# One core, two transformer blocks: the transposed copies of the second direction's inverse are taken by VectorE, and the attention's parts are dealt out in twos and ones

## The chip, the core and the metric

The kernel runs on one core of a Trainium2 chip. A core has five engines that run side by side and meet only in semaphores: TensorE (PE, matmuls, with PEld for its weight loads), VectorE (DVE), ScalarE (ACT), GpSimd (POOL) and SyncE (SP, which here only issues DMAs). Matmuls write PSUM (eight banks of 128 partitions by 512 float32), VectorE and ScalarE carry results from there to SBUF. The metric is device time in microseconds, lower is better: the median of the runs. Before the change three runs gave 1783.94 us (1781.68 to 1788.37).

## The reference

Two blocks follow each other. The first is a two-layer token mixer with pooling, dilated attention and a convolutional feed-forward net, over 256 tokens of width 1024. The second takes its output together with 256 context tokens and computes

```
h   = rms_norm(x) * (1 + scale) + shift;      p = h @ w_in            # for latents and context
a   = hgrn2_mixer(...)                        # gated linear attention, 4 heads, both directions
b   = rwkv7_mixer(...)                        # delta rule, 4 heads of 64, both directions
c   = neighbourhood_attention(...)            # 8 heads of 64, window and context keys, softmax
x   = x + g1 * (concat(a, b, c) @ w_out)
x   = x + g2 * hierarchical_moe(rms_norm(x))  # 32 experts, weights of some 200 MB
```

The delta rule is a recurrence over 512 tokens in each direction (context first, then latents):

```
sa = s @ kk_t
s  = s * w_t - sa * ak_t + v_t * k_t
y  = s @ r_t
```

The change touches b for the second direction (backwards over the tokens) and the order in which b and c are interleaved. Nothing of what is computed changes.

## The kernel before

**The tiles.** The delta rule is computed in chunks of 64 tokens, eight to a direction. Four groups g = 2*dr + pr hold the two directions dr and the two pairs of heads pr. For each chunk and head the kernel needs the inverse X of a unit triangular 64x64 matrix (made of LT) and its transpose XT. It is built up in levels: blocks of 2, 4, ... 64 rows. A level n has two stages of the list GROUP_STAGES (line 242 on):

- `MXn`: TensorE computes T1 = LT times X (`to_heads`, its records stand at L1649) and turns X with four transposes (`turned`, L1639; the job is named XV). T1 and XV are carried from PSUM to SBUF: w.T1 and w.XT, each 128x512 float32, by ScalarE (`take`, L2371).
- `XMXn`: TensorE waits for both copies and computes the update XU (`to_parity`, L1622; in the last level XTU by `heads64`, L1612), and VectorE merges it into X or XT under a mask (`copy_predicated`, L3069 and L3071).

Before the levels stands `products` (L1632, L1622, L1612), behind them `G`, `H` and `Psi`, whose products are taken by ScalarE too; in H, TensorE waits for G's take before it multiplies PH. The last result is GT of group 3, which the state recurrence behind the mixer (L1938) and the weight stream wait for.

**The attention.** "near" is the neighbourhood attention: eight pairs p of two heads, six parts each, 50 steps in all (`NA_STEPS`), done one part at a time:

- part 0: TensorE computes the logits ns of both heads (L1758), VectorE scales the first head's, adds the bias, finds the maximum and negates it (L2968, L2970, L2972, L2973). It waits until the previous pair has left the buffer nL, that is for the transposes nt.
- part 1: VectorE does the second head's logits; ScalarE takes the exponential of the first (L2410); TensorE computes the previous pair's output no (L1766), which VectorE copies (L2982).
- part 2: ScalarE, exponential of the second head. Part 3: VectorE, the reciprocal of the sums (L2986). Part 4: ScalarE scales both heads (L2416). Part 5: TensorE transposes the probabilities, nt (L1774), and ScalarE takes them (L2371).

**The order.** Every engine runs its instructions in the order of its program. `mixer_steps()` writes one list, MIXER_STEPS, which all the engines walk: the 56 steps of `GROUP_STEPS` (for each direction, for each stage, pair of heads 0, then 1), and behind step n so many attention parts as `NEAR_AT[n]` says. Steps 0 to 27 are the first direction, steps 28 to 55 the second. `group_jobs()` lists the PSUM results of a stage with the engine that empties each; from it `taken_order()` counts the semaphore values and `second_banks()` deals the PSUM banks (a job takes the bank whose last user is emptied first in the list). TensorE's `fill` waits for the earlier users of the bank.

**Behind the mixer** SyncE waits until GT of group 3 is in PSUM and then loads w_out (L1284), and after it the experts' weights in blocks of 2 MB (L1312), each as soon as the place it goes to is free; some of the places are held by the rest of the mixer, up to L3221, L3238, L3250 and L3263. The mixture of experts works through eight turns of four experts with these blocks.

Of the kernel before, what the change touches and what calls it, by code (L numbers as in the profile page):

```python
# [187 lines left out]
NCH = T2 // CH  # L188
# [54 lines left out]
GROUP_STEPS = [(stage, 2 * dr + pr) for dr in range(2) for stage in GROUP_STAGES for pr in range(2)]  # L243
# [7 lines left out]
def mixer_steps():  # L251
# [27 lines left out]
    for n, group_step in enumerate(GROUP_STEPS):  # L279
# [5 lines left out]
        if group_step == ("MX2", 1):  # L285
            steps.append(("vtok", 0))
        for _ in range(NEAR_AT[n]):
            steps.append(("near", i))
# [5 lines left out]
NA_PAIRS, NA_PARTS = 8, 6  # L294
NA_STEPS = NA_PAIRS * NA_PARTS + 2
ROPES_AT = {2: 0, 4: 1, 6: 2, 8: 3}
NEAR_AT = [int(n > 8 and n % 2 == 1) if n < 28 else 1 + int(n % 5 in (0, 3)) for n in range(len(GROUP_STEPS))]
MIXER_STEPS = mixer_steps()


def group_jobs(stage, g):

    if stage == "gates":
        return [("wz", g, "act"), ("az", g, "act")]
    if stage == "products":
        return [("LT", g, "act"), ("L1", g, "act"), ("ta", g, "act"), ("M2T", g, "dve"), ("tk", g, "act"), ("tkk", g, "act"),
                ("NN", g, "dve")]
    if stage == "G":
        return [("W2", g, "act")]
    if stage == "H":  # L310
        return [("G", g, "act"), ("H", g, "act"), ("HN", g, "act"), ("PH", g, "dve")]
    if stage == "Psi":
        return [("PS", g, "act"), ("GT", g, "act")]
    n = int(stage[-1])
    if stage[0] == "M":
        return [("T1", 8 * g + n, "act"), ("XV", 8 * g + n, "act")]
    return [("XU", 8 * g + n, "dve")] if n < 5 else [("XTU", 8 * g + n, "dve")]


# [193 lines left out]
def build(nc, d, out):  # L513

    ctx = ExitStack()
    with ctx:
# [3 lines left out]
        def sem(name):  # L520
            return ctx.enter_context(nc.semaphore(name))
# [76 lines left out]
        act = R[:, mark:mark + FT * S].rearrange("p (f s) -> p f s", s=S)  # L598
# [310 lines left out]
        w = ahead[0]  # L909
# [3 lines left out]
        w = ahead[1]  # L913
# [8 lines left out]
        def inputs_of(g):  # L922

            return (work if g < 2 else ahead)[g % 2]
# [55 lines left out]
        dve_emptied2 = sem("dve_emptied2")  # L980
# [29 lines left out]
        def wait_full2(eng, job):  # L1010

            eng.wait_ge(full2, JOB2[job] + 1)

        def wait_emptied2(eng, job):

            who, n = EMPTIED2[job]
            eng.wait_ge(act_emptied2 if who == "act" else dve_emptied2, n)
# [1118 lines left out]
        def _(act_eng):  # L2136
# [41 lines left out]
            for l in range(DEPTH):  # L2178
# [30 lines left out]
                else:  # L2209
                    for j in range(4):  # L2210
                        t, half = j // 2, j % 2
# [28 lines left out]
                for g in range(4):  # L2240
                    b = bank[JOB[("pool", g)] % 4]
# [35 lines left out]
                for j in range(11):  # L2277
                    wait_full(a, l, ("up", j))
                    high(l, SPLIT[("up", j)] + 2)
                    b = bank[JOB[("up", j)] % 4]  # L2280
# [41 lines left out]
            for j in range(4):  # L2322
                t, c = j // 2, slice((j % 2) * 512, (j % 2 + 1) * 512)
# [8 lines left out]
            def full_bank(job):  # L2332
                wait_full2(a, job)
                if job[0] in PLACE:
                    return place2(*job)
                return pair2(*job) if job[0] in QUADS else bank2(*job)
# [19 lines left out]
            def take(job, dst, func=ACT.Copy, scale=1.0, n=512, split=None):  # L2356
                b = full_bank(job)
                if job[0] in PLACE:
                    dst = dst.rearrange("p (n b) t -> p b n t", b=2)
                elif job[0] == "L1":  # L2360
                    dst, b = dst.rearrange("p (n b) t -> p b n t", b=2), b.rearrange("p b (n t) -> p b n t", t=64)
                elif job[0] in QUADS:
                    dst = dst.rearrange("p (b n) t -> p b (n t)", b=2)
                elif job[0] == "XV":
                    dst = dst.rearrange("p (b n) t -> p n b t", b=2)
                    b = b.rearrange("p (n b t) -> p n b t", n=NCH // 2, b=2)
                else:
                    b = b[:, 0:n]
                    if split:
                        b = b.rearrange("p (c s) -> p c s", c=split)  # L2370
                a.activation(dst, b, func, scale=scale).then_inc(act_emptied2, 1)  # L2371
# [63 lines left out]
            def group_step(stage, g):  # L2435
                dr, pr = g // 2, g % 2
                w = work[pr]
                if stage == "gates":
                    x = inputs_of(g)
                    for name, dst, vec in (("wz", x.sw, "rwkv_w0_2"), ("az", x.aa, "rwkv_a0_2")):  # L2440
                        c = VEC2[vec][0] + g
                        b = full_bank((name, g))
                        a.activation(dst, b, ACT.Sigmoid, bias=cols2[:, c:c + 1]).then_inc(act_emptied2, 1)
                    if g == 3:
                        wait_emptied2(a, ("b", 7))
                        a.activation(pB_g, pB_g, ACT.Sigmoid).then_inc(th_ready, 1)
                elif stage == "products":
                    take(("LT", g), w.LT[:, :, :], scale=-1.0)
                    take(("L1", g), w.X[:, :, :], scale=-1.0)
                    take(("ta", g), w.alpt[:, :, :])  # L2450
                    take(("tk", g), w.kapt[:, :, :], split=NCH)
                    wait_emptied2(a, ("M2T", g))
                    take(("tkk", g), w.kht[:, :, :])
                elif stage == "G":
                    take(("W2", g), w.W2[:, :, :])
                elif stage == "H":
                    take(("G", g), w.G[:, :, :])
                    take(("H", g), w.Hfull[:, :, :], scale=-1.0)
                    take(("HN", g), Hn[:, g, :, :], n=S, scale=-1.0, split=LCH)
                elif stage == "Psi":  # L2460
                    take(("PS", g), Psi[:, g, :, :], split=NCH)
                    take(("GT", g), GT[:, g, :, :], n=S, split=LCH)
                elif stage[0] == "M":
                    take(("T1", 8 * g + int(stage[-1])), w.T1[:, :, :])
                    take(("XV", 8 * g + int(stage[-1])), w.XT[:, :, :])

            for step, g in MIXER_STEPS:
                if step == "proj":
# [9 lines left out]
                elif step == "level" and LEVELS[g] >= COPY_FROM:  # L2478
                    n = LEVELS[g]
                    for j in range(4):  # L2480
# [3 lines left out]
                        b = full_bank(("lev", 4 * g + j)).rearrange("p (h s) -> p h s", h=4)  # L2484
# [51 lines left out]
            for j in range(4):  # L2536
                half, t = j // 2, j % 2
# [42 lines left out]
        def _(v):  # L2580
# [113 lines left out]
            for l in range(DEPTH):  # L2694
# [74 lines left out]
                for g in range(4):  # L2769
                    b = bank[JOB[("pool", g)] % 4]  # L2770
# [49 lines left out]
                for j in range(11):  # L2820
# [4 lines left out]
                    b = bank[JOB[("up", j)] % 4]  # L2825
# [43 lines left out]
                for j in range(4):  # L2869
                    t, half = j // 2, j % 2  # L2870
# [18 lines left out]
            def full_bank(job):  # L2889
                wait_full2(v, job)  # L2890
                return bank2(*job)
# [157 lines left out]
            def group_step(stage, g):  # L3049
                dr, pr = g // 2, g % 2  # L3050
                w = work[pr]

                if stage == "products":
                    wait_emptied2(v, ("L1", g))
                    v.copy_predicated(w.X[:, :, :], merge(0, 1 - dr), idb).then_inc(inverse_begun, 1)
                    v.tensor_tensor(n4(w.M2T), b4(("M2T", g)), mask4(0, dr), ALU.mult).then_inc(dve_emptied2, 1)
                    if g == 0:
                        v.wait_ge(nbias_ready, 1)
                    v.tensor_tensor(NN[:, g, :, :, :].rearrange("p a c t -> p (a c) t"), b3(("NN", g)), mask(1, dr), ALU.mult)\
                        .then_inc(dve_emptied2, 1)  # L3060
                elif stage == "H":

                    v.tensor_tensor(h4(PhiT[:, g, :, :]), inputs_of(g).ends.rearrange("p (n b) t -> p b n t", b=2), b4(("PH", g)), ALU.subtract)\
                        .then_inc(dve_emptied2, 1)
                    wait_emptied2(v, ("PH", g))
                elif stage[0] == "X":
                    n = int(stage[-1])
                    if n < 5:
                        v.copy_predicated(n4(w.X), merge4(n, 1 - dr), b4(("XU", 8 * g + n))).then_inc(dve_emptied2, 1)  # L3069
                    else:  # L3070
                        v.copy_predicated(w.XT[:, :, :], merge(n, dr), b3(("XTU", 8 * g + n))).then_inc(dve_emptied2, 1)  # L3071

            for step, g in MIXER_STEPS:
# [25 lines left out]
                elif step == "carry":  # L3099
                    wait_full2(v, ("kcT", 1))  # L3100
                    level_f(0)
                    for j in range(2):
                        b = full_bank(("hs", j))
                        v.tensor_tensor(hst[:, j, :, :], b[:, 0:A_W].rearrange("p (r m) -> p r m", r=2),
                                        ones_blk.unsqueeze(1).broadcast_to([P, 2, P]), ALU.mult).then_inc(dve_emptied2, 1)
                elif step == "diag":
                    for par in range(2):
                        b = full_bank(("diag", par))
                        v.tensor_copy(at3[par], b.rearrange("p (h s) -> p h s", h=4)).then_inc(dve_emptied2, 1)
                    wait_emptied2(v, ("diag", 1))  # L3110
                elif step == "level":
                    level_f(g + 1)
                    for j in range(4 if LEVELS[g] < COPY_FROM else 0):
# [3 lines left out]
                        b = full_bank(("lev", 4 * g + j))  # L3117
# [15 lines left out]
                elif step == "qsum":  # L3133
                    for j, dst in enumerate((nst[0:8, 0, :], nst[0:8, 1:3, :].rearrange("p a s -> p (a s)"))):
                        b = full_bank(("qs", j))
# [16 lines left out]
                elif step == "rope":  # L3152
                    x = (cq, cq, ck, ck)[g][:, 2 * (g % 2):2 * (g % 2) + 2, 0:S]
                    tr = nPT[:, 0, :, :].rearrange("p k s -> p (k s)").rearrange("p (i s) -> p i s", i=2)
                    b = full_bank(("rope", g)).rearrange("p (i s) -> p i s", i=2)
# [51 lines left out]
            for i in range(1, 7):  # L3207
                b = full_bank(("st", i))[:, 0:256].rearrange("p (g t) -> p g t", g=4)
# [44 lines left out]
            for j in range(4):  # L3253
                half, t = j // 2, j % 2
# [18 lines left out]
            b = full_bank(("rt", 0))  # L3273
# [56 lines left out]
            b = full_bank(("pos", 0))  # L3330
# [166 lines left out]
```

## Time and profile before

| what | us |
|---|---|
| median of three runs | 1783.94 |
| profiled execution | 1787.01 |
| its span, first to last instruction | 1785.2 |
| PE / DVE / ACT busy | 1574.3 / 839.8 / 652.5 |
| mean granted TensorE clock | 0.952 of 2.4 GHz |
| stretch 1213.74 to 1282.24, second direction: PE / DVE / ACT busy | 58.77 / 32.91 / 47.80 of 68.50 |

Times inside the profile are microseconds from the span's start. A timeline row gives the start, the time taken, the engine, line, operation, output and input, and in brackets the idle time of the engine just before it with what ended that. Two instructions of an engine that follow closely overlap, so that their starts lie closer than their lengths. A chain row gives the start and the share of one piece of the chain of work that ended last.

### The profile page before, as it was taken

What the parts mean: (1) busy time and instruction counts of PE and PEld (TensorE: products, weight loads), DVE (VectorE), ACT (ScalarE), POOL (GpSimd) and SP (SyncE); (2) the same over time, 40 slices, a digit from 0 to 9 for tenths busy, and PEclk for the clock granted to TensorE, in tenths of its full rate; (3) what the DMA queues carried; (4) which work ended last, traced back from release to release, by engine and by line L of the source; (5) the groups of instructions that cost most, each with busy time, mean ns of one, the idle gap of its engine ahead of it and who ended that gap; (6) DMA issues with size and microseconds to landing.
All of it is one profiled execution on the core that took longest, in us unless ns stands there. A gap on an engine that the chain in (4) does not pass through costs nothing.

```text
span 1785.2 us, 31410 instructions
## 1 busy us (share of the span) xinstructions
PE 1574.3 (88%) x13883; PEld 1259.2 (71%) x13883; DVE 839.8 (47%) x1127; ACT 652.5 (37%) x850; POOL 135.6 (8%) x105
## 2 busy tenths in 40 slices
PE   8999999999999999999998999988899765765576
PEld 7999998998799999899987987666654222212221
DVE  4444566665544455666656685885433101110111
ACT  4345545544344443455536223566512000000000
POOL 0600000000051000000001462000000000000000
PEclk9999999999999999999999999999999878788779
DMA  8553457755666525678552341000299999999998
GB/s 309 195 189 119 142 207 253 284 189 191 213 242 239 189 71 180 229 284 291 189 165 82 96 114 36 24 3 3 91 416 407 423 423 427 426 425 424 427 426 325
DMA packets 132323, 418.28 MB, mean 234 GB/s; under 512 B 14186, under 2 KB 35501, under 8 KB 113762
## 3 DMA queue, kind: packets, MB, share of 16 engines
q1 hardware_dynamic: 131762, 416.14, 61.5%
q8 instruction: 106, 1.74, 0.4%
q10 hardware_dynamic: 432, 0.22, 0.0%
q14 instruction: 23, 0.19, 0.0%
HBM read 414.45 MB, written 1.89 MB: 233 GB/s over the span
## 4 chain that ended last, share of the span: by engine, by line
PE 59%; DMA 19%; DVE 10%; ACT 6%; SPq 3%; issue 3%; DVEq 0%; ACTq 0%
PE ps_q L1423 17%; DMA R<-w_exp_down 17%; PE ps_p L1423 16%; SPq L1312 3%; PE ps_s L1538 3%; PE ps_t L1538 3%; ACT w_high L2147 2%; PE ps_p L1594 2%; PE ps_t L1594 2%; PE ps_s L1594 2%; DVE w_low L2639 1%; PE ps_q L1594 1%; PE ps_s L2086 1%; PE ps_t L2086 1%; DMA wring<-w_up 1%
## 5 line engine op out<-in xcount | busy, mean ns | idle before, releaser
L2639 DVE TENSOR_TENSOR w_low<-wring,w_high 128x2048 fp32r<-128x2048 f32 (+1 forms) x127 | 287.6, 2264 | 296.5 <-ACT w_high L2147 296.0
L2147 ACT ACTIVATE w_high<-wring 128x2048 fp32r<-128x2048 f32 (+1 forms) x127 | 236.3, 1860 | 325.2 <-PE ps_q L1423 147.4
L2069 PE MATMUL ps_q<-R 128*32 128x512 f32 x640 | 138.6, 712 | 107.3 <-DMA wring<-w_exp_up 64.8
L2069 PEld LDWEIGHTS ps_q<-R 128*32 128x32 f32 x640 | 34.4, 128 | 199.8 <-issue 128.6
L1423 PE MATMUL ps_q<-x_high,w_high 128*128 128x256 f32 x864 | 173.6, 282 | 1.3 <-DVEq L2690 1.3
L1423 PE MATMUL ps_q<-x_low,w_high 128*128 128x256 f32 x864 | 172.3, 281 | 0.0
L1423 PE MATMUL ps_q<-x_high,w_low 128*128 128x256 f32 x864 | 171.3, 279 | 0.0
L1423 PE MATMUL ps_p<-x_high,w_high 128*128 128x256 f32 x736 | 147.7, 282 | 2.2 <-DVEq L2690 1.9
L1423 PE MATMUL ps_p<-x_low,w_high 128*128 128x256 f32 x736 | 146.7, 281 | 0.0
L1423 PE MATMUL ps_p<-x_high,w_low 128*128 128x256 f32 x736 | 145.9, 279 | 0.0
L2069 PE MATMUL ps_q<-wring,R 128*32 128x512 f32 x384 | 138.4, 710 | 0.0
L1423 PEld LDWEIGHTS ps_q<-x_high,w_high 128*128 128x128 f32 x864 | 131.4, 189 | 5.2 <-issue 3.4
L1423 PEld LDWEIGHTS ps_q<-x_high,w_low 128*128 128x128 f32 x864 | 132.4, 188 | 0.0
L1423 PEld LDWEIGHTS ps_q<-x_low,w_high 128*128 128x128 f32 x864 | 131.8, 188 | 0.0
L3374 DVE TENSOR_TENSOR R<-ps_q,R 128x512 f32<-128x512 f32 x8 | 5.5, 693 | 241.8 <-PE ps_q L2069 241.8
L1423 PEld LDWEIGHTS ps_p<-x_high,w_high 128*128 128x128 f32 x736 | 111.9, 189 | 7.0 <-issue 4.6
L1423 PEld LDWEIGHTS ps_p<-x_high,w_low 128*128 128x128 f32 x736 | 112.8, 188 | 0.0
L1423 PEld LDWEIGHTS ps_p<-x_low,w_high 128*128 128x128 f32 x736 | 112.2, 188 | 0.0
L2636 DVE TENSOR_TENSOR w_low<-wring,w_high 128x2048 fp32r<-128x2048 f32 x22 | 50.4, 2292 | 58.1 <-ACT w_high L2145 58.1
L3416 POOL TENSOR_TENSOR R<-R 128x542 f32<-128x542 f32 (+3 forms) x20 | 38.7, 1936 | 475.6 <-ACT R L2183 474.2
L2086 PE MATMUL ps_s<-R 128*32 128x512 f32 x192 | 41.5, 760 | 33.7 <-DMA R<-w_exp_down 28.2
L2145 ACT ACTIVATE w_high<-wring 128x2048 fp32r<-128x2048 f32 x22 | 42.1, 1916 | 69.1 <-PE ps_t L1538 56.2
(802 smaller groups left out, 3018.3 us busy)
## 6 DMA issues: line engine op xcount, KB each, us to landing
wring<-w_in SPq DMA_DIRECT2D x29, 2048.0 KB, 8.2
R<-w_exp_up SPq DMA_DIRECT2D x24, 2048.0 KB, 37.2
R<-w_exp_down SPq DMA_DIRECT2D x23, 2048.0 KB, 44.4
wring<-w_up SPq DMA_DIRECT2D x22, 2048.0 KB, 8.0
R<-w_exp_gate SPq DMA_DIRECT2D x16, 2048.0 KB, 34.7
wring<-w_exp_gate SPq DMA_DIRECT2D x16, 2048.0 KB, 33.0
wring<-w_ada SPq DMA_DIRECT2D x12, 2048.0 KB, 10.1
wring<-w_down SPq DMA_DIRECT2D x10, 2048.0 KB, 7.8
```

The source lines that it names most:

```text
L1312: sp.dma_start(dst, src).then_inc(loaded[s], 16)
L1423: mm = pe.matmul(b[:, i * S:(i + 1) * S], left, right, start=k == 0 and m == 0 and i == 0, stop=k == last and m == 2, skip_group_check=True)
L1538: mm = pe.matmul(down_bank[j], left, ww[:, kk, half * 512:(half + 1) * 512], start=i == 0 and kk == 0 and m == 0, stop=i == N_DOWN - 1 and ...
L1594: mm = pe.matmul(b[:, i * width:(i + 1) * width], left, right, start=k == 0 and m == 0 and i == 0, stop=k == KT - 1 and m == 2, skip_group ...
L2069: mm = pe.matmul(banks8[2 + which][q, :], xg[:, k, q], weight(u, k), start=k == 0, stop=k == KT - 1)
L2086: mm = pe.matmul(banks8[5 + half][q, :], hidT[:, k, q], ww(u)[:, half * 512:(half + 1) * 512], start=k == 0, stop=k == D_EXP // P - 1)
L2145: a.activation(down_high(l, job[1]), down_rows(l, job[1], wring), ACT.Copy).then_inc(w_high_ready, 1)
L2147: a.activation(high_of(l, job), half_block(l, job, wring), ACT.Copy).then_inc(w_high_ready, 1)
L2636: v.tensor_tensor(down_rows(l, job[1], w_low), down_rows(l, job[1], wring), down_high(l, job[1]).bitcast(F32), ALU.subtract).then_inc(w_lo ...
L2639: v.tensor_tensor(half_block(l, job, w_low), half_block(l, job, wring), high_of(l, job).bitcast(F32), ALU.subtract).then_inc(w_low_ready, 1)
L3374: v.tensor_tensor(hid, banks8[3], sg, ALU.mult).then_inc(moe_hid, 1)
L3416: chain(g_eng.tensor_tensor(dst[:, :, 0:m], src[:, :, 0:m], src[:, :, w:w + m], ALU.add))
```

## The change

Two edits. In the second direction (g of 2 or more) XV is emptied by VectorE with a `tensor_copy` in place of ScalarE's `take`; this is so at all five levels and for both pairs of heads, ten copies. And `NEAR_AT` for steps 28 to 55 is written anew: 1, 1, then six times 2, 2, 1, 1, then 1, 1. Before, it was 1 + (n % 5 in (0, 3)): from step 28 on 2, 1, 2, 1, 1, 2, 1, 2, 1, 1, 2 and so on. Both lists hold 40 parts in these steps.

```
-NEAR_AT = [int(n > 8 and n % 2 == 1) if n < 28 else 1 + int(n % 5 in (0, 3)) for n in range(len(GROUP_STEPS))]
+NEAR_AT = [int(n > 8 and n % 2 == 1) for n in range(28)] + [1, 1] + 6 * [2, 2, 1, 1] + [1, 1]
+assert len(NEAR_AT) == len(GROUP_STEPS)
...
 def group_jobs(stage, g):
     if stage[0] == "M":
-        return [("T1", 8 * g + n, "act"), ("XV", 8 * g + n, "act")]
+        return [("T1", 8 * g + n, "act"), ("XV", 8 * g + n, "act" if g < 2 else "dve")]
...
 # ScalarE's group_step
                 elif stage[0] == "M":
                     take(("T1", 8 * g + int(stage[-1])), w.T1[:, :, :])
-                    take(("XV", 8 * g + int(stage[-1])), w.XT[:, :, :])
+                    if g < 2:
+                        take(("XV", 8 * g + int(stage[-1])), w.XT[:, :, :])
...
 # VectorE's group_step
+                elif stage[0] == "M" and g >= 2:
+                    job = ("XV", 8 * g + int(stage[-1]))
+                    b = full_bank(job).rearrange("p (n b t) -> p n b t", n=NCH // 2, b=2)
+                    v.tensor_copy(w.XT.rearrange("p (b n) t -> p n b t", b=2), b).then_inc(dve_emptied2, 1)
```

With the new list a level's four steps always carry the same six parts of one pair: MXn of pair of heads 0 has parts 0 and 1, MXn of 1 has parts 2 and 3, XMXn of 0 has part 4, XMXn of 1 has part 5. Pair 1's part 5 moves from behind the first `products` step to behind the second; pair 2 starts one step later than before (at the first MX1 step); pair 7 has parts 0 to 3 in G, part 4 and 5 in H. Since the jobs change their order, `second_banks()` deals the PSUM banks from step 28 on anew.

## Rows read from the trace of the kernel before

**Rows 1.** The page: the chain that ended last, by engine.
```profile
PE 59%; DMA 19%; DVE 10%; ACT 6%; SPq 3%; issue 3%; DVEq 0%; ACTq 0%
```

**Rows 2.** Windows, behind the mixer: length, engines' busy (x instructions), PEclk, DMA share, GB/s.
```profile
1339.00:1785.00 446.00, 291.28 (x1946) 106.97 (x1945) 67.77 (x191) 41.27 (x71) 0.00 (x0) 0.84 0.99 414
```

**Rows 3.** SP's queue: its timeline, then its waits (us in total, times, longest).
```profile
1282.27 1.08 SPq L1284 DMA_DIRECT2D wring<-w_out  x2
...
SPq L1312 <- DVE R L3263: 23.3, 2, 12.0
```

**Rows 4.** Windows from one pair's first logits to the next pair's, then the tail.
```profile
1226.77:1234.91 8.14, 7.01 (x168) 5.07 (x172) 4.82 (x12) 6.01 (x12) 0.00 (x0) 1.00 0.02 4
1234.91:1244.36 9.45, 8.28 (x202) 6.06 (x204) 4.72 (x12) 7.35 (x14) 0.00 (x0) 1.00 0.01 2
1244.36:1253.25 8.89, 7.07 (x168) 5.09 (x172) 4.83 (x13) 6.12 (x12) 0.00 (x0) 1.00 0.01 4
1253.25:1263.60 10.35, 8.39 (x168) 5.84 (x172) 4.74 (x12) 6.34 (x12) 0.00 (x0) 0.84 0.01 2
1263.60:1271.20 7.60, 7.02 (x164) 5.39 (x168) 4.82 (x13) 5.46 (x11) 0.00 (x0) 1.00 0.01 2
1271.20:1282.24 11.04, 9.85 (x350) 8.50 (x352) 4.86 (x12) 8.21 (x18) 0.00 (x0) 1.00 0.02 4
```

**Rows 5.** TensorE's timeline through one level (pair 5).
```profile
1250.88 0.69 PE L1649 MATMUL ps_p<-wring 64*64 64x64 f32 x32
1251.50 0.66 PE L1639 MATMUL ps_t<-ident,wring 128*128 128x128 f32 x4
1252.09 0.69 PE L1758 MATMUL ps_q<-R 64*128 64x512 f32 x1
...
1258.51 0.63 PE L1774 MATMUL ps_q<-ident,R 128*128 128x128 f32 x4 [1.96 <-ACT R L2416]
...
1259.68 1.12 PE L1649 MATMUL ps_t<-wring 64*64 64x64 f32 x32
```

**Rows 6.** VectorE's timeline in the same level.
```profile
1253.25 0.42 DVE L2968 SCALAR_TENSOR_TENSOR R<-ps_q,R 128x256 f32<-128x256 f32 x1 [3.81 <-PE ps_s L1758]
...
1254.84 0.42 DVE L2968 SCALAR_TENSOR_TENSOR R<-ps_s,R 128x256 f32<-128x256 f32 x1
...
1256.42 0.28 DVE L2982 COPY xs<-ps_q 128x128 f32<-128x128 f32 x1
...
1257.38 0.17 DVE L2986 RECIPROCAL R<-R 128x2 f32<-128x2 f32 x1
```

**Rows 7.** ScalarE's timeline in the same level.
```profile
1256.54 0.72 ACT L2410 ACTIVATE R<-R 128x512 f32<-128x512 f32 x1 [0.77 <-DVE R L2973]
...
1257.64 1.33 ACT L2416 ACTIVATE R<-R 128x512 f32<-128x512 f32 x2 [0.29 <-DVE R L2986]
```

**Rows 8.** Line L3109, a VectorE copy of a full PSUM bank: duration ns min/median/max.
```profile
L3109 DVE COPY wring<-ps_t x1: 682/682/682, 1017.0 to 1017.0; 128x512 f32<-128x512 f32 x1
```

**Rows 9.** The chain in order of time, pair 3's second exponential.
```profile
1237.81 1.15 ACT wring L2371 x2
1238.96 0.71 ACT R L2410 x2
```

**Rows 10.** TensorE's timeline, pair 1's transposes between the two products steps.
```profile
1220.18 1.24 PE L1774 MATMUL ps_t<-ident,R 128*128 128x128 f32 x8 [0.94 <-ACT R L2416]
```

**Rows 11.** The tail: pair 7's logits to GT of group 3, TensorE, and ScalarE's take.
```profile
1270.04 0.69 PE L1758 MATMUL ps_p<-R 64*128 64x512 f32 x1
...
1273.92 1.08 ACT L2371 ACTIVATE wring<-ps_p 128x512 f32<-128x512 f32 x2 [0.20 <-PE ps_p L1632]
...
1274.57 0.69 PE L1649 MATMUL ps_s<-wring 64*64 64x64 f32 x32 [0.25 <-ACT wring L2371]
...
1279.54 1.24 PE L1774 MATMUL ps_q<-ident,R 128*128 128x128 f32 x8 [0.68 <-ACT R L2416]
...
1281.80 0.44 PE L1639 MATMUL ps_t<-ident,wring 128*128 128x128 f32 x2
```

## The prediction

> **What bounds the kernel now.** I read the page first, then windows, then the queue of SyncE, then the chain and the timelines of one level. The page's chain gives PE 59% and DMA 19% over the whole span [rows 1], but the edits lie in steps 28 to 55, 1213.7 to 1282.2 us, so only that stretch and what hangs on its end matter. From 1339 to the end the DMA engines are busy 0.99 of the time at 414 GB/s [rows 2]: that part is a stream of weights and can't be hurried, only begun earlier or later. It begins when GT of group 3 is in PSUM: SyncE issues w_out at 1282.27, and the blocks after it wait for parts of the mixer's rest, the longest 12.0 us for L3263 [rows 3]. All of these come behind GT of group 3 in the order of the programs. So I take it that a shift of this one event moves the end of the kernel by the same amount, and everything below is about that event, now at 1282.24 (a window's end in rows 4, the last piece in rows 11).
>
> In the stretch no engine is full: TensorE is busy 7.07 of 8.89 us in an ordinary level, VectorE 4.83 and ScalarE 6.12 [rows 4]. The level is set by a chain through the attention. In pair 5: logits of both heads on VectorE from 1253.25, the second head's at 1254.84 [rows 6]; the second exponential at 1256.54, released by VectorE and not by ScalarE's other work; reciprocal 1257.38; scaling 1257.64 [rows 6, 7]; transposes nt at 1258.51 after 1.96 us in which TensorE had nothing to do [rows 5]; then T1, XV and the next pair's logits, since these stand behind nt in TensorE's order: 0.62 + 0.59 + 1.16 = 2.37 us from 1250.88 to 1253.25 one level earlier [rows 5, 6]. From the T1 at 1250.88 to the T1 at 1259.68 it is 8.80 us [rows 5]: that is one turn of the chain, and neither take of T1 or XV is on it.
>
> **Edit one: XV from ScalarE to VectorE.** ScalarE loses ten takes; two in a row last 1.15 [rows 9], so 0.57 each. VectorE gains ten copies of 128x512 from PSUM. This copy exists in the trace in the first gated mixer at 0.68 us [rows 8]; the new one writes the same size in runs of 64, for which no row exists, so I bound it by 0.57 below and by twice 0.68 = 1.36 above, and take 0.68. By the Trainium skill ("VectorE: DVE Perf Modes", the section on the TRN2 errata) such a copy costs VectorE 120 + 512 cycles at 0.96 GHz, an estimate of 0.66 us, and ScalarE 172 + 512 at 1.2 GHz, 0.57: the rule speaks against the move, the trace has 0.68, and if all ten were on the path it would be 1 us lost.
>
> Where do the copies lie? That of head pair 0 comes before the first logits on VectorE; XV ends on TensorE 1.09 us ahead of them, since ns is computed in between [rows 5], and 0.68 fits. That of head pair 1 comes behind both logits and the copy of no: with L the first logits' start, these take 1256.42 - 1253.25 + 0.2 = 3.4, so the copy lies at L+3.4 to L+4.1. Behind it on VectorE waits the reciprocal, whose input is ready at L+4.13 (1257.38 - 1253.25): hidden by 0.05. On TensorE XU of head pair 1 waits for it, runs 0.62 us from L+4.2 to L+4.8, and nt behind it needs the scaling, L+5.26: hidden by 0.45 us. So the copy costs nothing at 0.68, up to 0.6 per level at 1.36 (over all five levels 3 us).
>
> What does it give back? Only where a take holds up an exponential. In pair 3 the second exponential stands behind T1's and XV's take and starts at 1238.86 to 1238.96, where its logits were ready at 1238.1 [rows 9]: that level lasts 9.45, 0.65 more than a turn of 8.80. In the others there is 0.1 or nothing.
>
> **Edit two: the attention's parts.** The gain of 0.65 in pair 3 is met by losses, since two levels before were shorter than 8.80: 8.14 from pair 2 to 3 and 7.60 from 6 to 7 [rows 4]. There the old list put nt and the next logits ns next to each other, without T1 and XV (1.21) between. The new list has T1 and XV between them in every level. Level by level:
>
> - Start: pair 1's nt no longer stands between the products steps, where TensorE waited 0.94 for the scaling [rows 10]; but pair 2's logits now come behind T1 and XV. Pair 2: 1226.77 - 0.94 + 1.21 = 1227.04.
> - Pairs 2 to 6: four turns, 4 x 8.80 = 35.2, so pair 6's logits start at 1262.24 and its nt ends 6.43 later (1259.68 - 1253.25), at 1268.67. Before it ended at 1270.1 [rows 11], but with a stretch of half clock (below).
> - Tail, from nt of pair 6 (call it N) to GT: before 12.2 us (1270.04 to 1282.24), in it waits of 0.25, again 0.25, and 0.68 [rows 11]. After: W2 of head pair 0 moves behind nt, +0.62. Pair 7's parts 1 and 2 are both in G, so on ScalarE the second exponential now stands ahead of the take of G (before it stood behind it, and the take began at 1273.92 with TensorE waiting 0.25 [rows 11]). Logits start at N + 0.62 + 1.16 = N+1.78, the exponential at 3.3 later, N+5.1, and ends with its accumulator at N+5.9; G is taken by N+6.5. TensorE is out of work at 1274.57 - 0.25 - 1270.04 + 0.62 = N+4.9: a new wait of 1.6. The two scalings (1.33 [rows 7]) then stand ahead of the take of the other G: a wait of about 0.5. Tail: 12.2 + 0.62 - 1.18 + 2.1 = 13.7.
>
> GT is then at 1268.67 + 13.7 = 1282.4, against 1282.24. That would be +0.1 us, with one difference left: the clock.
>
> **The clock.** From pair 5 to 6 the granted clock is 0.84 and the level lasts 10.35, 1.5 more than a turn; T1 takes 1.12 in place of 0.69 [rows 4, 5]: half clock, the level of 1.2 GHz, after a level in which TensorE stood still for 1.96 us. My turns are clean of it. TensorE's waits don't get fewer (1.96 a level, as in pair 5), so I expect such a stretch again. Where it falls decides its price: 1.5 if on nt, T1, XV and ns, about nothing if in the slack. I take the middle, 0.8. Sum: +0.1 + 0.8 = +0.9 us; with both ends +0.1 to +1.6, and with the copy at its upper bound up to +4.7.
>
> The profiled execution (1787.01, span 1785.2) would become 1787.9. It lies 3.1 above the median of the runs; the shift is put on the median: 1783.94 + 0.9 = 1784.8.
>
> **The rivals.** A measurement of this kernel tells about 0.5%, 8.9 us, from no change; the three runs lie 6.7 apart.
>
> - *Forecast, chance 0.5:* the chain through the attention sets the levels, both edits nearly cancel, 1784.8, own range 1783 to 1788.
> - *ScalarE is on the path, 0.25:* If the levels are in fact set by ScalarE (the waits in front of L1622 and L2410 are small but in nearly every level), each of the five loses one take, 5 x 0.57 = 2.9, and if TensorE's wait of 0.68 for the scaling goes [rows 11] without the new one, 0.7 more: 1783.9 - 3.6 = 1780.3. For it: 9.45 in pair 3 [rows 4]. Against it: in pair 5 ScalarE was idle 0.77 before the exponential [rows 7].
> - *Nothing moves, 0.13:* the bank table or an order of waits that I misjudge eats the 0.1 and 0.8 alike: 1783.9.
> - *Slower through the clock, 0.12:* TensorE now waits about 2 us in each of the levels and 2.1 in the tail. If each such wait draws a stretch of half clock that falls on nt, T1, XV and ns, it is 1.5 each: with three in place of one 1783.9 + 1.6 + 3.0 = 1788.5, and with six, one for each of the five levels and the tail, 1783.9 + 1.6 + 7.5 = 1793.0. It decides against the forecast from the second stretch on, and reaches 0.5% only with the sixth. For it: in rows 4 one level in five had it. By the Trainium skill ("TensorE: Matmul & The Clock Gate", A second HAM failure mode) frequent short idle gaps between groups of matmuls are enough to make the clock swing between its two levels; the trace has one such swing in this stretch.
>
> **How the numbers follow.** The likeliest case gives 1784.8. The range reaches to the second and the fourth case and over the spread of the runs: 1779 to 1790. Beyond 0.5% on the fast side (1775.0) there is nothing but chance in measuring: 0.03. On the slow side (1792.9) the clock's far end and a copy at its bound: 0.04. Within: 0.93.
>
> **What would show it.** In the profile after: the ten copies at 0.68 each on VectorE; windows from logits to logits all near 8.8, with the first and last no longer short; ScalarE's second exponential released by VectorE in every level; TensorE waiting 1.5 or so for G's take behind L2410; no wait for nt's scaling at the very end; GT of group 3 and w_out's issue within 2 us of 1282.3 and 1282.27; the weight stream after it as long as before. The forecast is wrong if XU waits for VectorE long enough that nt is late, if levels come below 8.5, or if the end moves otherwise than GT does.

## The result: 0.35% slower, with the profile after

The changed kernel takes 1791.26 us (median of 10 runs, 1788.14 to 1793.75) against 1784.31 for the kernel before (10 runs, 1781.68 to 1788.37): a ratio of 1.0035, 95% interval 1.0025 to 1.0046, or 7.0 us more. The forecast was 1784.8 with a range of 1779 to 1790, so the time lies 1.3 us beyond the range. The profiled execution took 1791.08, its span 1789.3; the one of before took 1787.01, which lies 2.7 above its median, so the two traces show only 4.1 of the 7.0.

The changed kernel has more lines, so line numbers have moved: L3071 is now VectorE's new copy of XV and L3075 a merge, L1623 the updates XU, L1650 and L1640 T1 and XV, L1759 and L1775 the logits and the transposes.

The windows of the kernel after, cut like [rows 4] from one pair's first logits to the next pair's and then to w_out's issue (length, busy time of the engines with instructions, PEclk, DMA share, GB/s):

```profile
1225.29:1234.10 8.81, 7.14 (x166) 5.12 (x168) 6.11 (x15) 5.20 (x10) 0.00 (x0) 1.00 0.01 2
1234.10:1244.36 10.26, 8.52 (x166) 6.17 (x168) 6.11 (x15) 5.24 (x10) 0.00 (x0) 0.83 0.01 2
1244.36:1254.61 10.25, 8.52 (x166) 6.16 (x168) 6.11 (x14) 5.24 (x10) 0.00 (x0) 0.83 0.01 3
1254.61:1264.86 10.25, 8.51 (x166) 6.15 (x168) 6.11 (x15) 5.24 (x10) 0.00 (x0) 0.83 0.01 2
1264.86:1273.08 8.22, 7.35 (x162) 5.57 (x164) 5.45 (x14) 5.19 (x10) 0.00 (x0) 1.00 0.01 2
1273.08:1284.83 11.75, 9.64 (x350) 8.49 (x352) 4.86 (x12) 8.09 (x18) 0.00 (x0) 1.00 0.02 4
```

The first level took 8.81, the turn that the forecast had worked out, and the fifth 8.22 (6.43 + 1.78 by the forecast's own terms). The three between took 10.25 each, with a granted clock of 0.83. TensorE's timeline through the second of them answers to [rows 5]:

```profile
1248.51 0.69 PE L1623 MATMUL ps_q<-wring 64*64 64x64 f32 x32 [1.32 <-DVE wring L3071]
1249.62 0.63 PE L1775 MATMUL ps_t<-ident,R 128*128 128x128 f32 x4 [0.42 <-ACT R L2417]
1250.24 1.08 PE L1775 MATMUL ps_p<-ident,R 128*128 128x128 f32 x4
1251.25 1.13 PE L1650 MATMUL ps_s<-wring 64*64 64x64 f32 x32
1252.31 1.11 PE L1640 MATMUL ps_p<-ident,wring 128*128 128x128 f32 x4
1253.36 0.79 PE L1759 MATMUL ps_t<-R 64*128 64x512 f32 x1
```

XU of head pair 1 waits 1.32 us for VectorE's copy of XV (L3071), the transposes 0.42 for the scaling. Right behind these two waits the clock falls to half: the second head's transposes take 1.08 in place of 0.63, T1 1.13 in place of 0.69, XV 1.11 in place of 0.66. These, and the next logits, are the pieces of TensorE that lie on the attention's chain. The granted clock in three equal windows, placed on this point of three levels, 10.3 us apart:

```profile
1240.30:1243.70 3.40, 3.40 (x42) 2.42 (x42) 0.50 (x1) 1.58 (x3) 0.00 (x0) 0.55 0.00 0
1250.60:1254.00 3.40, 3.40 (x44) 2.37 (x42) 0.54 (x1) 1.54 (x3) 0.00 (x0) 0.56 0.02 5
1260.80:1264.20 3.40, 3.40 (x42) 2.42 (x42) 0.48 (x1) 1.59 (x3) 0.00 (x0) 0.56 0.03 5
```

So the half clock comes at the same place of each level, 1.2 of 2.4 GHz for nearly all of the 3.4 us. By the Trainium skill ("TensorE: Matmul & The Clock Gate", A second HAM failure mode) short idle gaps between groups of matmuls can make the clock swing; the trace agrees, with waits of 1.32 and 0.42 us ahead of each of the three stretches. It doesn't show that such waits are enough: the first level had waits of 0.96 and 0.42 and kept its full clock.

VectorE's copies are as assumed: L3071 in its timeline in the same level, behind both logits and the copy of no, and the reciprocal behind it. It answers to [rows 6]:

```profile
1247.53 0.28 DVE L2984 COPY xs<-ps_q 128x128 f32<-128x128 f32 x1
1247.73 0.68 DVE L3071 COPY wring<-ps_t 128x512 f32<-128x512 f32 x1
1248.50 0.17 DVE L2988 RECIPROCAL R<-R 128x2 f32<-128x2 f32 x1
```

In the tail, the first row of the next view (TensorE) shows the new wait for G's take, 1.68, which answers to the 0.25 in [rows 11]; below, SyncE's queue issues w_out at 1284.86, against 1282.27 in [rows 3].

```profile
1277.72 0.69 PE L1650 MATMUL ps_t<-wring 64*64 64x64 f32 x32 [1.68 <-ACT wring L2372]
```

```profile
1284.86 1.00 SPq L1285 DMA_DIRECT2D wring<-w_out  x2
```

From pair 2's first logits to w_out it was 1282.27 - 1226.77 = 55.50 and is 1284.86 - 1225.29 = 59.57: 4.1 us more. The second direction happened to start 1.2 us earlier in this execution (the row below, against 1213.74), and from its start to pair 2's logits it is 12.74 against 13.03, so these logits come 1.5 earlier in all.

```profile
1212.55 1.10 PE L1633 MATMUL ps_p<-R 64*64 64x128 f32 x32
```

Behind w_out it is 504.4 (1789.3 - 1284.86) against 502.9, 1.5 more. Of that 1.0 lies before the stream is steady: the first row is of before, the second of after, from w_out to the same block's issue (R<-w_exp_down, 1341.20 and 1344.77), with clocks of 0.94 and 0.91.

```profile
1282.27:1341.20 58.93, 53.50 (x584) 36.08 (x585) 21.51 (x65) 11.86 (x24) 0.00 (x0) 0.94 1.00 399
```

```profile
1284.86:1344.77 59.91, 54.46 (x584) 37.00 (x585) 21.52 (x65) 11.85 (x24) 0.00 (x0) 0.91 1.00 397
```

### The profile page after: what moved, and what is told of

The parts are those of the page before. It is cut to its first block, busy times and chain, and to the rows that moved or that the text cites. A ratio compares the mean times of both kernels' runs of the same rounds, so it can differ in the third digit from the quotient of the medians.

```text
span 1789.3 us, 31411 instructions
## 1 busy us (share of the span) xinstructions
PE 1576.3 (88%) x13883; PEld 1262.5 (71%) x13883; DVE 845.9 (47%) x1137; ACT 647.5 (36%) x840; POOL 135.6 (8%) x105
## 4 chain that ended last, share of the span: by engine, by line
PE 60%; DMA 18%; DVE 10%; ACT 6%; SPq 3%; issue 3%; DVEq 0%; ACTq 0%
PE ps_q L1424 18%; DMA R<-w_exp_down 17%; PE ps_p L1424 16%; SPq L1313 3%; PE ps_s L1539 3%; PE ps_t L1539 3%; ACT w_high L2148 2%; PE ps_p L1595 2%; PE ps_t L1595 2%; PE ps_s L1595 2%; DVE w_low L2641 1%; PE ps_s L2087 1%; PE ps_q L1595 1%; PE ps_t L2087 1%; DMA wring<-w_up 1%
## 6 DMA issues: line engine op xcount, KB each, us to landing
wring<-w_ada SPq DMA_DIRECT2D x12, 2048.0 KB, 10.3
```

## The experiments

Each was run in five rounds beside the kernel before, whose medians in the three sets were 1784.55, 1784.53 and 1783.97. "Even list" is the changed kernel's 2, 2, 1, 1; "uneven list" that of before; "idle matmuls" are matmuls of 128x128 whose result is overwritten unread.

### The two edits apart

`a1_xv_only`: the changed kernel with the old list.

```
-NEAR_AT = ... + [1, 1] + 6 * [2, 2, 1, 1] + [1, 1]
+NEAR_AT = [int(n > 8 and n % 2 == 1) if n < 28 else 1 + int(n % 5 in (0, 3)) for n in range(len(GROUP_STEPS))]
```

> The first edit alone: XV of the second direction is copied by VectorE, the attention's parts are dealt as before. Order theory (my walk: the copy is hidden behind the attention's chain): a few tenths faster, 1783.5, pair 3's second exponential no longer behind XV's take and that level near 8.8 in place of 9.45. Clock theory (what costs is half-clock stretches that the even list draws): the uneven list is back, so again 1784, within 2 us of before, with one half-clock stretch or none in the five levels. If VectorE's copy were itself what costs: near 1791, as the changed kernel.

Measured: 1787.17, ratio 1.0016 (1.0007 to 1.0025), so 2.6 us slower than before. None of the expectations hit. Its profile has two levels of 10.7 us, the first of which is shown, and behind them one at full clock that takes 8.17 where it took 7.60 before [rows 4]:

```profile
1241.71:1252.43 10.72, 8.56 (x169) 6.20 (x172) 6.01 (x15) 5.23 (x10) 0.00 (x0) 0.84 0.01 3
...
1263.16:1271.33 8.17, 7.02 (x164) 5.39 (x168) 5.32 (x14) 5.01 (x10) 0.00 (x0) 1.00 0.01 2
```

In the first of them, in this order, VectorE's copy, merge and reciprocal, ScalarE's scaling and TensorE's transposes:

```profile
1245.07 0.68 DVE L3071 COPY wring<-ps_q 128x512 f32<-128x512 f32 x1
1245.67 0.72 DVE L3075 COPY_PREDICATED wring<-R,ps_p 128x512 f32<-128x512 uint8 x1
1246.28 0.15 DVE L2988 RECIPROCAL R<-R 128x2 f32<-128x2 f32 x1
```

```profile
1246.53 1.33 ACT L2417 ACTIVATE R<-R 128x512 f32<-128x512 f32 x2 [0.73 <-DVE R L2988]
```

```profile
1247.40 0.63 PE L1775 MATMUL ps_q<-ident,R 128*128 128x128 f32 x4 [0.85 <-DVE wring L3075]
```

In the uneven list the copy is thus not hidden. A merge stands between it and the reciprocal in VectorE's order, so the reciprocal comes 4.57 us after the first logits (1246.28 - 1241.71), where it comes 4.14 after them in the changed kernel, and the scaling and nt are late by the same 0.43. The profile puts nt's wait down to the second merge, which ended at about the same time, but nt starts 0.87 behind the start of the scaling as it does in the changed kernel (0.86), and its bank's last users are the logits, which had long left it. In the next two levels the copy stands between the two heads' logits and costs 0.57: 8.17 against 7.60 at full clock. The rest of the two long levels is half clock, about 1.4 in each. From pair 2's logits to w_out it makes 58.3 us against 55.5.

`a2_near_only`: the even list, XV taken by ScalarE (the two other hunks of the first edit undone too).

```
-        return [("T1", 8 * g + n, "act"), ("XV", 8 * g + n, "act" if g < 2 else "dve")]
+        return [("T1", 8 * g + n, "act"), ("XV", 8 * g + n, "act")]
```

> The second edit alone: the parts are dealt 2, 2, 1, 1, XV is taken by ScalarE as before. Clock theory: levels of one kind, each with about 2 us in which TensorE waits, draw half-clock stretches on the transposes, T1, XV and the next logits: 1789 to 1792, levels of 10.2 us in the profile. Copy theory (VectorE's copy is what costs): 1784 to 1786, levels of 8.8.

Measured: 1790.02, ratio 1.0030 (1.0019 to 1.0042). The even list alone brings most of the loss, 5.5 of the 7.0 by the medians, with two levels at half clock, one shown behind a level without it:

```profile
1234.73:1243.61 8.88, 7.06 (x166) 5.09 (x168) 4.71 (x12) 6.12 (x12) 0.00 (x0) 1.00 0.01 2
1243.61:1253.91 10.30, 8.49 (x166) 6.14 (x168) 4.72 (x12) 6.20 (x12) 0.00 (x0) 0.83 0.01 3
```

These two levels have the same waits, 0.77 and 0.76 ahead of XU and 1.05 ahead of the transposes, whose rows in both follow; the half clock comes in the second alone:

```profile
1240.07 0.63 PE L1775 MATMUL ps_t<-ident,R 128*128 128x128 f32 x4 [1.05 <-ACT R L2417]
...
1248.95 0.63 PE L1775 MATMUL ps_t<-ident,R 128*128 128x128 f32 x4 [1.05 <-ACT R L2417]
```

### Filling TensorE's waits

`a3_fill`: the changed kernel with idle matmuls in levels 1 to 4.

```
                     if n < 5:
                         b = fill("XU", 8 * g + n)
+                        if g == 2:
+                            keep_clock(b[:, 0, 0:P], ident[:, :], ident[:, :], 8)
...
                         b = fill("nt", 2 * p + hd)
+                        if hd == 0 and p >= 2:
+                            keep_clock(b[:, 0:P], ident[:, :], ident[:, :], 2)
```

> The changed kernel with idle matmuls added that nobody reads, in the second direction: eight of 128x128 in front of XU of head pair 0 in levels 1 to 4, two in front of the transposes nt from pair 2 on. They go where TensorE waits 1.3 and 0.4 us in each level, so they should delay nothing. Clock theory: no half-clock stretch in the levels, each 8.8 in place of 10.25, and 1791.3 - 3 x 1.45 = about 1787. Any theory of order or copies: as the changed kernel, 1791, or slower by what the added matmuls cost.

Measured: 1786.31, ratio 1.0011 (1.0002 to 1.0021). No level at half clock, but TensorE is now full in a level, 8.90 of 8.90:

```profile
1243.18:1252.08 8.90, 8.90 (x186) 7.31 (x188) 6.12 (x14) 5.08 (x10) 0.00 (x0) 1.00 0.01 2
```

The eight take 1.95 us, 0.24 each, and so don't fit in the wait of 1.3 that they were meant for. Against its own kernel before it is 1.8 us slower by the medians, where the changed kernel was 7.0. That the idle matmuls do work nobody needs and still give back about 5 us (4 by the ratios) leaves the order theories no room for the larger part.

`c3_fill_nt_only`: the second of the two hunks alone.

> The changed kernel with only the two idle matmuls in front of the transposes (the wait of 0.4 us), none before XU. TensorE keeps its wait of 1.3 us for VectorE's copy of XV in each level. If that longer wait is what draws the half clock: 1791, levels of 10.25 as before. If filling any wait is enough: 1787.

Measured: 1784.83, ratio 1.0009 (0.9999 to 1.0018). Two idle matmuls a level bring the difference to before from 7.0 us to 0.9 by the medians, by the ratios from 1.0035 to 1.0009, which is 4.6 us. All four levels have the turn of 8.80, though XU still waits for VectorE in each: 0.96 in the first, 1.32 in the others, of which one row stands first. The last row of the windows is the tail:

```profile
1246.31 0.69 PE L1623 MATMUL ps_q<-wring 64*64 64x64 f32 x32 [1.32 <-DVE wring L3073]
```

```profile
1233.36:1242.16 8.80, 7.48 (x170) 5.58 (x172) 6.11 (x15) 5.16 (x10) 0.00 (x0) 1.00 0.01 2
1242.16:1250.96 8.80, 7.48 (x170) 5.58 (x172) 6.12 (x14) 5.16 (x10) 0.00 (x0) 1.00 0.01 4
1250.96:1259.77 8.81, 7.50 (x170) 5.59 (x172) 6.12 (x15) 5.16 (x10) 0.00 (x0) 1.00 0.01 2
1259.77:1268.29 8.52, 7.65 (x166) 6.08 (x168) 5.44 (x13) 5.08 (x10) 0.00 (x0) 1.00 0.01 2
1268.29:1280.56 12.27, 10.16 (x354) 9.01 (x356) 4.86 (x12) 8.11 (x18) 0.00 (x0) 1.00 0.02 4
```

So "the longer wait draws it" fell and "filling any wait is enough" held, at 2 us below the 1787 expected for it. From pair 2's logits to w_out it is 56.00 us against 59.57 of the changed kernel, 3.6 less: the three stretches are gone (4.35), and the idle matmuls cost 0.3 in the level of 8.52 and 0.5 in the tail, where there was no wait for them. Its profile also has less behind w_out, 1781.9 - 1280.56 = 501.3, against 504.4 of the changed kernel; the clock from w_out on is 0.97 there:

```profile
1280.56:1339.00 58.44, 54.38 (x589) 36.07 (x590) 23.04 (x73) 13.69 (x25) 0.00 (x0) 0.97 1.00 400
```

`c2_near_only_fill`: the kernel of a2 with both hunks of a3.

> The second edit alone (parts 2, 2, 1, 1, XV on ScalarE) with the same idle matmuls as in the filled changed kernel (eight before XU of head pair 0, two before the transposes). The filled changed kernel gave 1786.3. Clock theory: no half-clock stretch in the levels, 8.9 each, and 1790.0 goes to 1786, the same as with XV on VectorE, since in this order the copy is hidden on either engine. Rival (the copies on VectorE cost on their own): 1785 or less, clearly below 1786.3.

Measured: 1785.60, ratio 1.0010 (0.9998 to 1.0023; one of 12 runs, at 2568.8, lies far from all others). Levels of 8.90, and a time between the 1786 of the clock theory and the 1785 of its rival. With the clock held, XV on ScalarE or on VectorE makes 0.7 us between the two kernels, and 0.1 when each is set against the kernel before in its own set (1.6 and 1.8 slower): not told apart.

`c1_xv_only_fill`: the kernel of a1 with the first hunk of a3.

> The first edit alone (XV on VectorE, parts dealt as before) with eight idle matmuls in front of XU of head pair 0 in levels 1 to 4, which had two levels of 10.7 us at half clock in its profile and 1787.2. Clock theory: those levels go to about 9.2, 3 us less: 1784.5. What stays above 8.8 is VectorE's own: its copy of XV holds up XU of head pair 1, whose merge holds the bank of the transposes. Rival (the 10.7 is all VectorE's): 1787.

Measured: 1785.66, ratio 1.0013 (1.0002 to 1.0025), 1.5 less than a1 and not the 3 expected: no half clock, but the two levels of 10.7 are 9.96 and 10.16 and not 9.2, since here the idle matmuls push XU of head pair 0 back, and with it the merge that stands ahead of the reciprocal.

```profile
1241.84:1251.80 9.96, 8.63 (x184) 6.80 (x188) 5.99 (x14) 5.19 (x10) 0.00 (x0) 1.00 0.02 3
```

It says that the clock was part of a1's loss. It also fills only the other wait, the one ahead of XU: that ended the half clock too, although the transposes still wait 1.33 us.

`b4_before_fill`: the kernel before with six idle matmuls in front of nt (the second hunk of a3, with 6).

> The kernel before with six idle matmuls in front of the transposes nt from pair 2 on, where TensorE waits 0.8 to 2.0 us. Clock theory: the one half-clock stretch in its levels (the level of 10.35) goes, 1 to 1.5 us less than before. Rival (in the kernel before the stretch falls in the levels only now and then, or comes from other waits): within 0.5 us of before.

Measured: 1784.96, ratio 0.9997 (0.9988 to 1.0006). The level at half clock is gone, 8.81 in place of 10.35, but others grew: six take some 1.4 us (0.24 each), too much for those waits, and the levels are 9.4, 9.6, 9.0 and 8.8. The time is the rival's, within 0.5 of before, and the reason is neither's. It shows only that filling is no gain where the filler is longer than the wait.

### The tail

`b1_tail`: the changed kernel with another end of the list.

```
+NEAR_AT = [int(n > 8 and n % 2 == 1) for n in range(28)] + [1, 1] + 5 * [2, 2, 1, 1] + [2, 0, 1, 2, 1, 2]
```

> The changed kernel with the last six entries of the list as 2, 0, 1, 2, 1, 2: pair 7's second exponential stands behind the take of G again, as in the kernel before; the levels are left even. Theory (the rest of the loss that the added matmuls didn't give back is the tail): TensorE's wait of 1.7 us for G's take goes to 0.25, a wait of 0.7 for the scaling comes, net 1.0 to 1.5 less, 1790. Rival (the rest is something else, such as the copies on VectorE): 1791.3 as the changed kernel.

Measured: 1790.46, ratio 1.0029 (1.0015 to 1.0042); 0.8 less than the changed kernel and not told apart from it. In the profile, from pair 7's logits to w_out, it is 11.24 against 11.78 (1284.86 - 1273.08): the tail's order costs 0.5 us, half or less of the 1.0 to 1.5 that I expected. The same three levels as in the changed kernel are at half clock, 10.16 or 10.17 each.

```profile
1274.24:1285.48 11.24, 9.72 (x350) 8.43 (x352) 4.86 (x12) 8.01 (x18) 0.00 (x0) 1.00 0.02 4
```

### A shorter chain

The chain holds T1 and XV only because the next logits stand behind them. `a4_joined` puts them next to nt:

```
+NEAR_AT = [int(n > 8 and n % 2 == 1) for n in range(28)] + [1, 2] + 5 * [1, 2, 1, 2] + [1, 0, 1, 2, 1, 2]
```

> XV on VectorE, and another list: 1, 2, then five times 1, 2, 1, 2, then 1, 0, 1, 2, 1, 2. Each pair's transposes are followed at once by the next pair's logits, without T1 and XV between, and pair 7's second exponential comes behind G's take. Order theory: one turn of the chain is 8.80 - 1.21 = 7.6 us in each level, the tail loses its new wait of 1.7: the weights' stream begins some 6 us earlier than in the kernel before, about 1779. Clock theory adds: TensorE waits under 1 us a level, so at most one half-clock stretch; if the clock falls in spite of it, 1781 to 1784.

Measured: 1781.04, ratio 0.9979 (0.9968 to 0.9990). No half clock in the levels, but 8.17 each and not 7.6: VectorE's copy of head pair 0's XV now stands between the two heads' logits.

`b2_joined_act`: the same list on the kernel before, a change of one line.

> The joined list (transposes and next logits side by side) with XV on ScalarE as before: one line changed against the kernel before. In the joined kernel with XV on VectorE a level took 8.17, and VectorE's copy of XV stood between the two heads' logits. Theory (VectorE's copy lengthens the chain by its 0.6 us per level): levels of 7.6, about 3 us less than that kernel's 1781.0, so 1778. Rival (ScalarE's two takes then stand before the exponential and cost as much): levels of 8.1, 1781.

Measured: 1780.13, ratio 0.9978 (0.9968 to 0.9987), levels of 8.24: the rival was right. ScalarE's takes of T1 and XV stand before the second exponential, which starts 3.95 us after the first logits, 0.65 later than the 3.3 in pair 5 of the kernel before. TensorE waits 1.06 us for the scaling in every level, and none is at half clock.

`b3_joined_act_rec`: b2 with idle matmuls in the recurrence.

```
...
+                if i in (4, 5):
+                    b = fill("st", i + 1)
+                    keep_clock(b[:, 0:P], ident[:, :], ident[:, :], 4)
                 wait_emptied2(pe, ("st", i))
```

> As the one before, and in the state recurrence behind the mixer four idle matmuls in each of the waits of 0.72 us for VectorE in steps 4 and 5, into the bank of the next step. Clock theory for the recurrence (half clock for 6.8 to 10.2 us there, in which the products take 1.12 in place of 0.68): the stretch gets shorter by 3.4, 1 to 2 us less than without. Rival (the half clock there comes from the wait of 2.3 to 2.8 us before, which is not filled): no change, within 0.5 us.

Measured: 1780.37, ratio 0.9986 (0.9976 to 0.9996), no change against b2. It is inconclusive: in b2's own profile there was no half clock in the recurrence to remove.

`c4_joined_half`: the joined list, XV of head pair 1 on VectorE, of head pair 0 on ScalarE (the lines of both engines changed to match).

```
-        return [("T1", 8 * g + n, "act"), ("XV", 8 * g + n, "act" if g < 2 else "dve")]
+        return [("T1", 8 * g + n, "act"), ("XV", 8 * g + n, "act" if g < 3 else "dve")]
```

> The joined list, with XV on ScalarE for head pair 0 and on VectorE for head pair 1. In the two joined kernels a level took 8.17 (VectorE's copy of head pair 0's XV stood between the two heads' logits) and 8.24 (ScalarE's takes of T1 and XV of head pair 1 stood before the second exponential). Here neither stands there: a level of 7.6 to 7.7, 3 us less than those, 1777 to 1778. If some other wait comes in its place (XU of head pair 1 behind VectorE's copy): 8.0 and 1779.5.

Measured: 1776.49, ratio 0.9966 (0.9951 to 0.9981), the fastest of all and 0.5 below what was expected: by the medians 7.5 us under the kernel before, by the ratio 6. One level of each of the three joined kernels, in this order:

```profile
1239.88:1248.06 8.18, 7.08 (x168) 5.10 (x172) 5.99 (x15) 5.31 (x10) 0.00 (x0) 1.00 0.01 4
```

```profile
1239.97:1248.21 8.24, 7.07 (x168) 5.08 (x172) 4.72 (x12) 6.19 (x12) 0.00 (x0) 1.00 0.01 2
```

```profile
1238.78:1246.47 7.69, 7.07 (x168) 5.09 (x172) 5.52 (x14) 5.64 (x11) 0.00 (x0) 1.00 0.02 4
```

TensorE is busy 7.07 us in each; only what lies on the chain differs. Here VectorE's take of XV is worth its 0.5 us a level, in a list in which ScalarE's take would stand in the way.

## Why the prediction was wrong

**What bounds the kernel: right.** The attention's chain sets the levels. The turn of 8.80 was met to 0.01 in the one level at full clock, and in all of c3; c4 took T1 and XV (1.21) off the chain and shortened a level by 1.1; a4 and b2 by 0.6, since in them a copy or a take came onto the chain.

**Edit one: right for the even list.** The copies take 0.68 to 0.69 as from [rows 8], the reciprocal follows them at once, and XU and nt start 4.15 and 5.26 after the first logits, for the forecast's 4.2 and 5.26. That XU of head pair 1 waits for them was foreseen, and so was that it costs nothing on the chain. It was said nowhere that this rests on the list: with the uneven one (a1) the copy costs 0.4 to 0.6 us in three of the levels.

**Edit two: right in sign, a little too dear.** The short levels of 8.14 and 7.60 are gone. The tail was reckoned at 11.9 from pair 7's logits (13.7 - 1.78) and is 11.75, with its wait of 1.68 for the 1.6 and a second of 0.43 for the 0.5 that were forecast. Clean of half clock the forecast put the loss at 0.1 + 1.5 = 1.6 us against a kernel before that is clean too; from pair 2's logits to w_out the profiles give 59.57 - 3 x 1.45 = 55.2 against 55.5 - 1.5 = 54.0, so 1.2. The start was misjudged: pair 2's logits were to come 0.27 later in the direction and come 0.29 earlier, so that from the direction's start the loss is 0.9.

**The clock: the step that failed.** It read: "so I expect such a stretch again. Where it falls decides its price: 1.5 if on nt, T1, XV and ns, about nothing if in the slack. I take the middle, 0.8." There were three, none in the slack, 1.45 each: 4.35 us where 0.8 was put. The slower rival was this mechanism and had 1788.5 for three stretches, but only 0.12 of the chance. What I missed is that the even list makes the levels alike: the same waits ahead of the same pieces on the chain, and in the changed kernel and in b1 three levels in a row with the same stretch. In the uneven list of before, the levels had waits of 1.13, 1.06, 0.77, 1.05 and 1.96 us at different distances, and one stretch. Filling the last wait ended it (c3), and with it went 4.6 to 6.1 of the 7.0 us, of which its profile shows 3.6 in the levels. That the stretches cost this is shown; what tips a level is not. Likeness alone doesn't: in a2 two levels with the same waits differ, b2's levels are alike, with a wait of 1.06 in each, and have none, and a1 has the uneven list and two.

**From GT to the end: not quite one to one.** I took the shift of GT as the shift of the end. The profiles have 1.5 us more behind w_out, with a lower clock in the state recurrence (0.91 against 0.94), and c3 has 3.1 less than the changed kernel, at 0.97. But with one profile of each kernel this decides nothing: over all fourteen the time behind w_out runs from 501.3 to 506.9, and a4, with every level at full clock, has 506.0. That the new levels cause the 1.5 isn't shown, and the one test of the recurrence (b3) met no such stretch. This part stays open.

The sum then: +1.2 for the order and -1.5 + 4.35 = +2.9 for the clock in the levels, together the 4.1 from pair 2's logits to w_out; +1.5 behind w_out; -1.5 ahead of pair 2's logits, 1.2 of it before the second direction. This gives the 4.1 between the two spans. The other 2.9 of the medians' 7.0 isn't seen in this pair of profiles; 2.7 is what the profiled execution of before lies above its median.

## What to carry to other kernels

Before you even out a schedule, look at where TensorE waits in the repeated unit and what comes right behind: half clock that fell once in the uneven schedule fell in three of four units of the even one here, and when the pieces behind it are on the chain, each stretch costs its full price. It can be tested cheaply by one or two idle matmuls in that wait, into a bank that is about to be overwritten, and they must fit in it: two did (c3), eight and six did not (a3, b4). And ask of each piece on the chain whether it is there only by its place in the program: moving the next logits ahead of T1 and XV, and giving each copy to the engine where nothing on the chain stands behind it, was worth 6 to 7.5 us.

## What was not expected of the hardware

- Half clock locked to the program: three stretches of about 3.4 us, 10.3 us apart, in three levels of 10.25, each behind waits of 1.32 and 0.42.
- A wait alone isn't what does it: c3 keeps the 1.32 in three levels and has a clock of 1.00, so filling only the 0.42 sufficed; c1 fills only the other wait and has 1.00 too; in a2 two levels with the same waits ran at 1.00 and 0.83.
- An idle matmul of 128x128 in float32 takes 0.24 us (eight in 1.95), a transpose of the same size 0.16 (four in 0.63).
- VectorE's copy out of a full PSUM bank into runs of 64 takes 0.68 to 0.69, as the plain one does.
